# Hybrid decoder step on one core: the local stage, the latent projections and the latent prompt attention as one program, and the order of PE's work within an item of the sample attention

## Chip, cores and metric

One Trainium2 chip (trn2), of which the kernel uses one core. The metric is the device time of one execution in microseconds (us). Engines are named as in the profile: PE (TensorE matmul), PEld (its weight load), DVE (VectorE), ACT (ScalarE), POOL (GpSimd), SP (SyncE, which here issues most transfers).

## The reference

One inference step of one decoder layer. 2048 prompt tokens and 8 samples of 8 new tokens each, with 8192 cached tokens per sample, pass one RMS norm and one input projection. Three kinds of attention follow: **A**, multi-head latent attention (8 heads, latent width 256, shared rotary key of 32); **B**, dilated windows (4 heads of 64, three patterns, 128 keys back each, combined by their softmax sums); **C**, cross attention to 256 memory tokens. The branches are gated, projected and added to the input. The part that the change touches, cut:

```python
q = einsum('bsr,rhd->bshd', rmsnorm(cq, q_a_norm), w_uq)      # 384 -> 8 heads x 96
q_rope = rope(q[..., 64:], pos); ckv = rmsnorm(ckv, kv_a_norm)
o_b = combine_dilations([dilated_prompt(qb, kb, vb, r, w // r) for w, r in ((128, 1), (512, 4), (2048, 16))])
o_c = cross_attend(qc, mk, mv)
# A, prompt: softmax over keys <= own position of (q_lat.ckv + q_rope.krope) * scale, times ckv
# A, sample: the same over 8192 cached tokens (ckv_past, kr_past, by page table) and the 8 new ones
```

## The kernel before

All products are made in 32-bit, and where full precision matters each operand is split into a rounded high part (`_hi`, fp32r) and the difference to it (`_lo`); `mm3` (L97-102) then makes three matmuls: high by high (L100), high by low (L101), low by high (L102).

`program` (L2871-2930) runs stages one behind another. Up to the prompt attention each stage has its own block, and between two blocks all five engines meet at a barrier; the last two stages (sample attention and output projection) share one. `Buffers.release` (L90-94) clears a stage's semaphores and adds a barrier. Within a block each engine has a written order of instructions, and counting semaphores release one engine's work by another's. SP's queue is in order as well: a wait in it holds every later transfer.

**Local stage**, `prompt_windows_and_memory` (L601-977): 64 steps `g` (16 of memory attention, then the patterns d16, d4, d1, 16 each), each on 128 query rows by 4 heads. A loop over `t` runs the parts of a step at fixed distances: `score(t)`, turning of the probabilities `turn(t-2)`, `value(t-3)`, `turn_back(t-4)`. After t = 63 the loop drains for five more turns, with fewer parts in each. SP's loop loads values ahead, and stores results of step t-4 (`store`). `load_ahead` (L703) loads the weights and the first latent chunk of the next stage into `ahead` (class `LatentWeights`, L576), and POOL splits them (`split_ahead`, L762). The last act of SP there is `stored_by(NG)`, a wait for all stores.

**Latent projections**, `prompt_latent_projections` (L1020-1408): four chunks `c` of 512 tokens, and 14 products of 128 x 512 in each: 4 values (`val`), 4 keys (`k_nope`), 6 queries (`Q_ORDER`: four without and two with rotation). Value and key products take six matmuls, query products nine. `acc` has seven banks in turn; ACT and DVE empty them by the table `ON_DVE` (the odd ones of the first eight products and the rotary two, the last in the order, on DVE). A rotary product costs DVE a shuffle, two multiplications and an addition (L1398-1406). SP loads, in this order ahead of chunk 0: the query chunk `load_cq(0)`, eight pieces of the rotary table (2 MB, `rot_loaded`), and then the latent rows of chunk 1. ACT and DVE split the first query chunk at the stage's start, DVE then waits for `rot_loaded` (L1367) ahead of its first eviction. Between products stand `side_step`s for the new sample tokens, which read six small loads. Per chunk SP stores keys, rotary queries (`store_rope`, L1007-1012: four transfers, whose outer dimension is 4 heads) and plain queries (`store_nope`, L1014-1017, one transfer) to memory, where the next stage reads them. Each result buffer is single: it is filled again when its store has landed. In the last chunk SP loads the first unit's keys and queries for the attention (L1145-1150) behind waits for all earlier stores and issues them last; the last stores of plain and rotary queries are left to the next block.

**Prompt attention**, `prompt_latent_attention` (L1411-1863): 32 units, each 256 queries by a pair of heads (8 units to a pair); queries are split by POOL (`split_q`, L1610), from unit 1 on. Unit 0's queries and the keys of the first pair are cast by ACT and subtracted by DVE: queries and key chunk 0 at the stage's start (L1775-1778, L1845-1850), key chunks 1, 2, 3 ahead of the first scores of units 1, 2 and 4 (`CHUNK_BEHIND`, L1548). The list `STEPS` gives one order of score, turn, value and back for all engines. On SP: key chunk 1, queries of unit 2, the last plain-query store, queries of unit 3, key chunk 2, the last rotary store, key chunk 3, and then two units ahead. DVE takes each row's masked scores (L1815), ACT the exponentials (L1755).

**Sample attention**, `sample_attention` (from L1889): 80 items, one after another; 64 of them are past items of 1024 cached tokens. PE's part of an item `n`: `score(n)` (L2133), which for a past item is latent products (L2166, tiles of 128 rows by 64 columns) and then rotary products (L2174, tiles of 64 by 64); `turn_probs(n-1)` (L2178-2186, 64 by 128), which turns the probabilities of the item before; `turn_keys(n+1)` (L2126, 64 by 128); `value(n-1)` (L2209-2225, 128 by 64). Keys are turned and evicted by ACT (L2274) and DVE (L2343), the turned probabilities by ACT (L2280) and DVE (L2374).

```python
2229    for n in range(N):
2230        score(n)
2231        if n:
2232            turn_probs(n - 1)
2233        if n + 1 < N:
2234            turn_keys(n + 1)
2235        if n:
2236            value(n - 1)
```

## Time and profile before

| | |
|---|---|
| median of 3 runs | 1977.24 us (1976.37 to 1979.61) |
| profiled execution | 1976.4 us |
| its span from first to last instruction | 1974.8 us |
| mean granted TensorE clock | 0.985 |
| PE busy | 1890.9 us, 96% |
| DVE, ACT, POOL busy | 53%, 45%, 22% |
| DMA packets | 192238, 270.80 MB, 137 GB/s on the mean |

The page gives busy time as a share of the whole span, and 40 slices of equal length (49 us) with the busy share and the granted clock of each. A view of windows gives the same for any stretch, a view of the timeline gives instructions in order: start, length, engine, line, operation, what it writes and reads, the tile, and in brackets the engine's idle time before it and what released it. `PEq` as a releaser is PE's own sequencer (a barrier or clearing), `SPq` an issue on SP's queue. A time in the text is one from the span's start.

### The profile page before, as it was taken

Reading aid. Unit: us, or ns where it says so; the run is one execution under the profiler, and the core shown is the slowest. Engines: PE = TensorE matmul, PEld = TensorE weight load, DVE = VectorE, ACT = ScalarE, POOL = GpSimd, SP = SyncE. Lnnn points to the kernel's source line nnn. Section 1 sums busy time; section 2 is a strip of 40 time slices with the busy share of each in tenths; the row PEclk is TensorE's granted clock in tenths of the full one; section 3 lists DMA queues with packets and bytes.
Section 4 is the critical chain, followed back from the end, with each engine's and each line's share of the span. In section 5 each row is a group of like instructions: output and inputs, shape, how many; then the busy total and the mean of one; then the engine's idle time right before and its main releaser. Section 6 shows DMA issues by size and latency. Waiting matters only on the chain. (4 is left out here: it accounts for less than half of the span.)

```text
span 1974.8 us, 47163 instructions
## 1 busy us (share of the span) xinstructions
PE 1890.9 (96%) x18076; PEld 1469.0 (74%) x18076; DVE 1047.8 (53%) x3035; ACT 886.8 (45%) x2043; POOL 425.1 (22%) x568
## 2 busy tenths in 40 slices
PE   7999999999989899999999799999999999999998
PEld 6989898766777667776677466666666678888886
DVE  4433434688844477667677455555556753223232
ACT  5222222688822355566556333343434553333332
POOL 0111111355013130134101222222222321211110
PEclk9999999999989899999999799999999999999999
DMA  8534343733465520112001598767784653333331
GB/s 299 155 105 120 100 125 94 216 98 124 141 167 161 162 76 18 46 38 68 26 18 52 169 298 230 222 222 228 241 234 143 207 205 107 102 96 102 119 101 52
DMA packets 192238, 270.80 MB, mean 137 GB/s; under 512 B 37176, under 2 KB 152328, under 8 KB 183128
## 3 DMA queue, kind: packets, MB, share of 16 engines
q1 hardware_dynamic: 172344, 170.27, 30.3%
q0 software_dynamic: 19712, 98.01, 14.4%
q8 instruction: 126, 2.06, 0.4%
q14 instruction: 56, 0.46, 0.1%
HBM read 212.99 MB, written 54.95 MB: 136 GB/s over the span
## 5 line engine op out<-in xcount | busy, mean ns | idle before, releaser
L100 PE MATMUL proj_acc<-proj_w_hi,proj_x_hi 128*128 128x512 f32 (+2 forms) x512 | 183.9, 359 | 10.8 <-DVE proj_x_lo L368 8.2
L101 PE MATMUL proj_acc<-proj_w_lo,proj_x_hi 128*128 128x512 f32 (+2 forms) x512 | 181.8, 355 | 0.0
L102 PE MATMUL proj_acc<-proj_w_hi,proj_x_lo 128*128 128x512 f32 (+2 forms) x512 | 181.8, 355 | 0.0
L1755 ACT ACTIVATE mla_probs<-mla_probs,mla_bias 128x256 f32<-128x256 f32 (+15 forms) x128 | 153.0, 1196 | 11.0 <-DVE mla_bias L1819 7.4
L1815 DVE CUSTOM_DVE_ANT_0 mla_probs<-mla_scores,keep_in_rms 128x512 f32<-128x512 f32 x192 | 124.8, 687 | 59.2 <-PE mla_scores L1673 59.0
L2280 ACT ACTIVATE dec_pT<-dec_outs 128x256 f32<-128x256 f32 x80 | 30.7, 384 | 228.6 <-PE dec_outs L2186 186.1
L2166 PE MATMUL dec_scores<-dec_keysT,sample_q_lat 128*64 128x256 f32 x1024 | 127.0, 388 | 3.3 <-ACT dec_probs L2294 2.2
L2374 DVE COPY dec_pT<-dec_p_turned 128x256 f32<-128x256 f32 x80 | 33.9, 424 | 171.5 <-PE dec_outs L2186 143.6
L100 PEld LDWEIGHTS proj_acc<-proj_w_hi,proj_x_hi 128*128 128x128 f32 x512 | 97.3, 190 | 21.8 <-issue 8.2
L2166 PEld LDWEIGHTS dec_scores<-dec_keysT,sample_q_lat 128*64 128x64 f32 x1024 | 74.4, 139 | 45.1 <-ACT dec_probs L2294 11.6
L2225 PE MATMUL dec_outs<-late_ckv,dec_pT 128*64 128x256 f32 x816 | 101.6, 388 | 5.1 <-DVE dec_pT L2374 4.9
L102 PEld LDWEIGHTS proj_acc<-proj_w_hi,proj_x_lo 128*128 128x128 f32 x512 | 97.2, 190 | 10.7
L101 PEld LDWEIGHTS proj_acc<-proj_w_lo,proj_x_hi 128*128 128x128 f32 x512 | 97.4, 190 | 10.2
L2343 DVE COPY dec_keysT<-dec_turned 128x512 f32<-128x512 f32 (+1 forms) x160 | 96.2, 642 | 10.3 <-PE dec_turned L2126 10.3
L1673 PE MATMUL mla_scores<-mla_k_hi,mla_qn_hi 64*128 64x512 f32 (+3 forms) x320 | 86.6, 455 | 13.5 <-DVE mla_lowest L1815 7.0
L2087 POOL DMA_INDIRECT late_ckv<-in_cache_ckv,sample_rows_of x51 | 48.4, 949 | 236.9 <-PE dec_outs L2225 225.2
L2274 ACT ACTIVATE dec_keysT<-dec_turned 128x512 f32<-128x512 f32 (+1 forms) x160 | 88.9, 557 | 21.9 <-PE dec_turned L2126 19.1
L900 ACT ACTIVATE win_probs<-win_probs,win_rec 128x256 f32<-128x256 f32 (+1 forms) x192 | 86.6, 453 | 21.5 <-DVE win_rec L939 20.9
L269 POOL DMA_DIRECT2D featT<-proj_featT x34 | 26.7, 784 | 309.2 <-DVE proj_featT L429 293.6
L431 DVE COPY proj_featT<-proj_tr 128x512 f32<-128x512 f32 x16 | 11.1, 691 | 151.6 <-PE proj_tr L490 151.6
L1698 PEld LDWEIGHTS mla_turned<-host_ident,mla_probs 64*128 64x128 f32 x2180 | 79.8, 139 | 15.1 <-ACT mla_probs L1755 7.9
L1698 PE MATMUL mla_turned<-host_ident,mla_probs 64*128 64x64 f32 x2180 | 84.1, 224 | 3.9 <-ACT mla_probs L1755 3.9
(466 smaller groups left out, 4933.7 us busy)
## 6 DMA issues: line engine op xcount, KB each, us to landing
win_v_tile<-wv_out SPq DMA_DIRECT2D x75, 128.0 KB
memory_x_raw<-in_xT SPq DMA_DIRECT2D x17, 512.0 KB, 5.1
proj_rows<-in_x SPq DMA_DIRECT2D x17, 512.0 KB, 4.1
featT<-proj_featT POOLq DMA_DIRECT2D x34, 256.0 KB
late_ckv<-in_xT SPq DMA_DIRECT2D x17, 512.0 KB, 6.6
late_ckv<-in_x SPq DMA_DIRECT2D x17, 512.0 KB, 4.3
y_out<-host_buf POOLq DMA_DIRECT2D x16, 512.0 KB, 6.5
dec_k_rows<-in_win_k SPq DMA_DIRECT2D x64, 96.0 KB
```

Of the source, the lines that this page charges most:

```text
L100: pe.matmul(out, lh, rh, start=start, stop=False)
L101: pe.matmul(out, lh, rl, start=False, stop=False)
L102: return pe.matmul(out, ll, rh, start=False, stop=stop)
L900: act.activation(pr, pr, ACT.Exp, bias=low[:, h:h + 1], scale=-1.0, accum_out=total[:, h:h + 1]).then_inc(exp_done, 1)
L1673: mm = pe.matmul(scores[:, at % 3, 0:n], lhs[rows, :], rhs[rows, :], start=a == 0, stop=a == len(parts) - 1)
L1698: mm = pe.transpose(turned[:, r % 2, lane, (kb * 2 * QB + w) * 64:(kb * 2 * QB + w + 1) * 64], probs[rows, u % 2, w, src * P:(src + 1) * P ...
L1755: act.activation(row, row, ACT.Exp, bias=bias[:, at:at + 1], scale=-1.0, accum_out=total[:, at:at + 1]).then_inc(exp_done, 1)
L1815: dve.tensor_tensor_reduce(probs[:, u % 2, w, c * CH:c * CH + wide], scores[:, n % 3, 0:wide], add, -MLA_SCALE, -LOWEST, ALU.add, ALU.min, ...
L2166: pe.matmul(scores[h * Q:(h + 1) * Q, r, 0:HALF * Q], q_lat[:, c, s, :], lanes_of(n, c, r)[:, h * HALF:(h + 1) * HALF, :], start=c == 0, s ...
L2225: mm = pe.matmul(outs[h * Q:(h + 1) * Q, 0:KVL], pT[:, u, j, h * Q:(h + 1) * Q], values[:, h * HALF + j, :], start=j == 0, stop=j == HALF - 1)
L2274: act.activation(lanes_of(n, c, 0), turned_of(n, c, 0), ACT.Copy).then_inc(k_act, 1)
L2343: dve.tensor_copy(lanes_of(n, c, 1), turned_of(n, c, 1)).then_inc(k_dve, 1)
```

## The change

What it does, in the order of the program:

- The three stages become functions that return their per-engine programs, and `program` puts them into one block. No barrier stands between them. `early.release()` goes; POOL clears the early stages' semaphores in the attention, behind unit 12 (`u == NI + 4`). The semaphores of the input projection are cleared (without a barrier) ahead of the block.
- Local stage: SP loads the first query chunk at step 10; POOL casts and subtracts it behind its last staging copy. PE makes the four value products of chunk 0 in the drain, behind `value(61)` to `value(63)` and one turn more, once all scores are masked. SP's wait for the stores goes to where chunk 0's `load_ckv(1)` has been issued.
- Projections: the division of the patterns' shares on DVE (`shares`) goes behind the fourth value product, the wait for the rotary table to the first rotary product. In the last chunk SP issues the first unit's loads ahead of the key store, behind waits for older stores; the third unit's queries behind it; and the last rotary and plain stores in the usual place. ACT casts the first unit's parts ahead of query product 0 (i = 8), DVE subtracts them ahead of product 9; the third key chunk is subtracted behind the last rotation.
- Attention: only key chunk 3 is left in `CHUNK_BEHIND`. SP begins with the queries of unit 3. The order of some buffers in SBUF changes, so that the early casts overwrite nothing in use, and keys are four tiles instead of two.
- Sample attention: for a past item n > 0, `turn_probs(n - 1)` stands between the latent and the rotary products of item n.

The diff, cut to its core ("..." marks what is left out):

```diff
@@ prompt_windows_and_memory: SP @@
+        def wait_stored(sp):
+            stored_by(sp, NG)
...
+                if w == 10:
+                    sp.dma_start(ahead.cq_raw[:], io["featT"].rearrange("(f p) t -> p f t", p=P)[:, FB_CQ:FB_CQ + ahead.QK, 0:ahead.CH]).then_inc(ahead.cq_loaded, 16)
                 if w in (8, 9):
...
-            stored_by(NG)
@@ POOL, behind the loop over the steps @@
+            pool.wait_ge(ahead.cq_loaded, 16)
+            pool.tensor_copy(ahead.cq_hi[:], ahead.cq_raw[:]).then_inc(ahead.cq_high, 1)
+            pool.wait_ge(ahead.cq_high, 1)
+            pool.tensor_tensor(ahead.cq_lo[:], ahead.cq_raw[:], ahead.cq_hi[:].bitcast(F32), ALU.subtract).then_inc(ahead.cq_low, 1)
@@ PE @@
                 if 0 <= t - 3 < NG:
                     value(t - 3)
+                if t == NG:
+                    pe.wait_ge(masked, H_B * NG)
+                if NG <= t < NG + 4:
+                    product(pe, 0, t - NG)
@@ prompt_latent_projections: SP @@
-            load_cq(0)
             for g in range(4):
                 sp.dma_start(cos[32 * g:32 * g + 32, :], io["rotT"][0:32, 0:SEQ]).then_inc(rot_loaded, 16)
...
                 if c == 0:
+                    before.wait_stored(sp)
                     sp.dma_start(cqT[:], feat[:, FB_CQ:FB_CQ + QK, new]).then_inc(new_loaded, 16)
...
-                sp.wait_ge(act_kept, kept_on_act(c, 7))
-                sp.wait_ge(dve_kept, kept_on_dve(c, 7))
                 if c == NCK - 1:
                     sp.wait_ge(ahead.shares_stored, 16)
                     sp.wait_ge(new_valued, DEC_B // 2)
                     sp.wait_ge(k_stored, 16 * c)
-                    sp.wait_ge(qn_stored, 16 * c)
-                    sp.wait_ge(qr_stored, 64 * c)
-                    sp.dma_start(host.k_raw[:, 0:host.CH], io["mla_k"][0:P, 0:host.CH]).then_inc(host.first_loaded, 16)
...
+                    sp.wait_ge(qn_stored, 16)
+                    sp.wait_ge(qr_stored, 64)
+                    first.load(sp)
+                sp.wait_ge(act_kept, kept_on_act(c, 7))
+                sp.wait_ge(dve_kept, kept_on_dve(c, 7))
                 sp.dma_start(io["mla_k"].rearrange("(g p) t -> p g t", p=P)[:, :, cols], k_nope[:]).then_inc(k_stored, 16)
                 if c + 1 < NCK:
                     load_cq(c + 1)
-                if c == NCK - 1:
-                    break
+                else:
+                    sp.wait_ge(qn_stored, 16 * c)
+                    sp.wait_ge(qr_stored, 64 * c)
+                    first.load_third(sp)
                 sp.wait_ge(roped, 2 * c + 2)
-                prompt.store_rope(sp, io, c, qr_stored)
+                prompt.store_rope(sp, io, c, qr_stored if c < NCK - 1 else prompt.qr_last_stored)
                 sp.wait_ge(act_kept, kept_on_act(c, PER - 1))
                 prompt.store_nope(sp, io, c)
@@ PE @@
+                    if c or i >= OUTS_V:
+                        product(pe, c, i)
@@ ACT @@
-            split_cq(0)
...
+                        if c == NCK - 1 and i == OUTS_V + OUTS_K:
+                            first.cast(act)
+                            act.wait_ge(projected, c * PER + i + 1)
@@ DVE @@
-            dve.wait_ge(rot_loaded, 128)
...
+                    if c == NCK - 1 and i == OUTS_V + OUTS_K + 1:
+                        first.split(dve)
                     dve.wait_ge(projected, c * PER + i + 1)
...
                         dve.tensor_copy(val[:, c * 4 + i, :, :].rearrange("p h n -> p (h n)"), src).then_inc(dve_kept, 1)
+                        if c == 0 and i == OUTS_V - 1:
+                            shares()
...
                         if n:
                             dve.wait_ge(roped, n)
+                        else:
+                            dve.wait_ge(rot_loaded, 128)
...
+            first.split_third(dve)
@@ prompt_latent_attention @@
-        CHUNK_BEHIND = {1: 1, 2: 2, 4: 3}
+        LAT_KEYS, LAT_ALL = 3 * 14 + 8, 4 * 14
+        CHUNK_BEHIND = {4: 3}
+
+        def load_first(sp):
+            sp.dma_start(k_raw[:, 0:CH], io["mla_k"][0:P, 0:CH]).then_inc(host.first_loaded, 16)
...
+        def load_third(sp):
+            sp.wait_ge(first_q_ready, 2)
...
+        def cast_first(act):
+            act.wait_ge(host.first_loaded, 48)
+            act.wait_ge(prompt.projected, LAT_KEYS)
+            act.activation(qn_hi[:, 0, :], qn_raw[:, 0, :], ACT.Copy).then_inc(first_q_high, 1)
+            cast_first_k(act, 0)
+            act.activation(qr_hi[:, 0, :], qr_raw[:, 0, :], ACT.Copy).then_inc(first_q_high, 1)
+            cast_first_k(act, 1)
+            cast_first_k(act, 2)
...
-            load_first_k(1)
-            load_q(2)
-            prompt.store_nope(sp, io, SEQ // CH - 1)
             load_q(3)
-            load_first_k(2)
-            prompt.store_rope(sp, io, SEQ // CH - 1, prompt.qr_last_stored)
             sp.wait_ge(masks, 1)
-            load_first_k(3)
+            sp.wait_ge(prompt.k_stored, 16 * SEQ // CH)
+            sp.dma_start(k_raw[:, 3 * CH:], io["mla_k"][0:P, 3 * CH:]).then_inc(first_k_loaded[3], 16)
@@ sample_attention @@
+        def turned_within(n):
+            return n and ITEMS[n][0] == "past"
...
+            if within:
+                turn_probs(n - 1)
             pe.wait_ge(kr_turned, l + 1)
...
             score(n)
-            if n:
+            if n and not turned_within(n):
                 turn_probs(n - 1)
@@ program @@
-            early.release()
+            with nc.Block() as block:
+                @block.sync
+                def _(sp):
+                    windows.sync(sp)
+                    projections.sync(sp, stored, first)
+                    attention.sync(sp)
...
```

## Rows read from the trace of the kernel before

**Rows 1.** The page: busy time of the engines, and PE's granted clock in 40 slices.

```profile
PE 1890.9 (96%) x18076; PEld 1469.0 (74%) x18076; DVE 1047.8 (53%) x3035; ACT 886.8 (45%) x2043; POOL 425.1 (22%) x568
...
PEclk9999999999989899999999799999999999999999
```

**Rows 2.** Windows: length, busy by engine (PE to POOL), granted clock, DMA share, GB/s.

```profile
545.00:550.00 5.00, 3.68 (x52) 2.59 (x48) 2.10 (x5) 0.98 (x2) 0.00 (x0) 1.00 0.16 56
555.00:560.00 5.00, 5.00 (x16) 3.95 (x15) 0.70 (x1) 2.22 (x3) 2.31 (x2) 0.66 1.06 287
565.00:570.00 5.00, 3.02 (x11) 2.15 (x10) 2.26 (x4) 0.60 (x1) 0.00 (x0) 0.86 1.07 281
```

**Rows 3.** Timeline, end of the local stage to chunk 1: start, length, instruction, [idle before, releaser].

```profile
544.71 0.71 PE L849 MATMUL win_turned<-host_ident,win_probs 64*128 64x64 f32 x16 [0.61 <-ACT win_probsT L907]
...
552.73 0.77 PE L100 MATMUL lat_acc<-ahead_wv_hi,ahead_ckv_hi 128*128 128x512 f32 x1 [2.99 <-PEq L646]
...
568.49 0.72 PE L100 MATMUL lat_acc<-lat_cq_hi,ahead_wq_hi 128*128 128x512 f32 x1 [1.98 <-DVE prompt_val L1387]
...
575.69 0.39 PE L100 MATMUL lat_acc<-lat_cq_hi,ahead_wq_hi 128*128 128x512 f32 x1
...
576.37 0.39 PE L100 MATMUL lat_acc<-lat_cq_hi,ahead_wq_hi 128*128 128x512 f32 x1
...
582.49 0.39 PE L100 MATMUL lat_acc<-ahead_wv_hi,ahead_ckv_hi 128*128 128x512 f32 x1
```

**Rows 4.** Timeline, end of the latent projections to unit 3 of the prompt attention.

```profile
677.15 0.42 ACT L1776 ACTIVATE mla_qn_hi<-host_buf 128x256 fp32r<-128x256 f32 x1 [1.76 <-PEq L94]
...
679.58 0.48 PE L1673 MATMUL mla_scores<-mla_k_hi,mla_qn_hi 64*128 64x128 f32 x2 [4.82 <-DVE mla_qr_lo L1850]
...
681.05 0.29 DVE L1815 CUSTOM_DVE_ANT_0 mla_probs<-mla_scores,mla_mask 128x128 f32<-128x128 f32 x1 [1.53 <-PE mla_scores L1673]
...
690.33 0.69 DVE L1803 TENSOR_TENSOR mla_k_lo<-host_buf,mla_k_hi 128x512 fp32r<-128x512 f32 x1 [0.83 <-ACT mla_k_hi L1746]
...
691.69 0.32 PE L1673 MATMUL mla_scores<-mla_k_hi,mla_qn_hi 64*128 64x128 f32 x1 [1.92 <-DVE mla_lowest L1815]
...
696.15 0.47 PE L1673 MATMUL mla_scores<-mla_k_hi,mla_qn_hi 64*128 64x512 f32 x1
```

**Rows 5.** Timeline of issues, releases and rotations around it, with one row of windows.

```profile
650.32 3.65 SPq L1012 DMA_DIRECT2D mla_qr<-prompt_q_rope  x4
...
654.02 1.58 SPq L1017 DMA_DIRECT2D mla_qn<-prompt_q_nope  x1
...
667.51 0.60 ACT L1312 ACTIVATE prompt_q_nope<-lat_acc 128x512 f32<-128x512 f32 x1 [5.71 <-DMA mla_qn<-prompt_q_nope]
...
663.00:665.00 2.00, 2.00 (x10) 1.65 (x10) 0.25 (x1) 0.00 (x0) 0.00 (x0) 1.00 0.26 102
...
666.65 0.73 DVE L1398 STREAM_SHUFFLE lat_swapped<-lat_acc 128x512 f32<-128x512 f32 x1
...
670.73 0.01 DVE L1398 LOAD_MASK_SELECT lat_swapped<-lat_acc  x1 [1.05 <-PE lat_acc L102]
...
672.72 0.69 DVE L1406 TENSOR_TENSOR prompt_q_rope<-lat_turned_cos,lat_turned_sin 128x512 f32<-128x512 f32 x1
...
700.57 0.40 POOL L1618 CAST mla_qn_hi<-host_buf 128x256 fp32r<-128x256 f32 x1 [11.48 <-DMA host_buf<-mla_qr]
```

**Rows 6.** Sample stage: timeline of one item, and PE's waits by releaser (sum, count, longest).

```profile
1250.97 1.16 PE L2126 MATMUL dec_turned<-host_ident,late_ckv 64*128 64x64 f32 x32
...
1252.06 1.95 PE L2225 MATMUL dec_outs<-late_ckv,dec_pT 128*64 128x256 f32 x16
...
1255.66 0.43 PEld L2174 LDWEIGHTS dec_scores<-dec_krT,sample_q_rot 64*64 64x64 f32 x16 [0.38 <-issue]
...
1256.26 0.14 PEld L2186 LDWEIGHTS dec_p_turned<-host_ident,dec_probs 64*128 64x128 f32 x1 [0.17 <-issue]
...
PE dec_outs L2225 <- DVE dec_pT L2374: 7.1, 13, 0.8
```

307 lines of the change are left out of this document (164 added, 143 removed).

## The prediction

> **What bounds the kernel now.** I read the page first: its busy row and its clock row [rows 1]. PE is busy 96% of the span, but the granted clock dips in three places, and a matmul at the low clock counts as busy too. So the question at each place is what PE does there, which busy time alone does not tell. Then I read the windows around the two seams where one block ends and the next begins [rows 2], the timeline of the first seam [rows 3], that of the second [rows 4], the transfers in flight there [rows 5], and last the item of the sample stage [rows 6].
>
> At the first seam PE ends the local stage at 549.74 and starts the latent projections at 552.73: 2.99 us with nothing, and then 1.2 GHz (0.66 of full clock over 555 to 560). A second hole of 1.98 us at 566.5 has another cause: DVE stands before the rotary table's transfer with banks 1 and 3 unread behind it. The clock falls again (0.86, the matmul there 0.72 us long) [rows 2, 3].
>
> At the second seam PE ends at 674.77 and starts scoring at 679.58, 4.82 us later, released by the last of the first unit's splits. PE waits 1.92 us more at 691.69, because the split of the third key chunk stands in ACT's and DVE's queues ahead of the scores [rows 4].
>
> **The change, first seam.** Removed: the barrier; the wait for the table ahead of the first value product's eviction; the load and split of the first query chunk between the stages. Four value products move into the local stage's last steps. Everything PE does from 549.74 to 582.49, where chunk 1 begins, is the 14 products of chunk 0: 8 of six matmuls and 6 of nine, 102 in all. Three matmuls take 0.68 us at full clock (575.69 to 576.37, and ten such steps more make 582.49), so 102 take 23.1 us. They took 32.75. That leaves 9.6 us of holes and slow clock. In the local stage's tail PE also idles 0.61 us at 544.1 and 1.06 us in 545 to 549.74 (5.00 less 3.68 busy less the 0.26 of the hole) [rows 2, 3]; the four products can fill these. Sum: **-11.3 us**, chunk 1 beginning at 571.2. Bounds: if a hole of the size of the second stays with its slow clock (1.98, and some 1.7 for eight matmuls at 0.43 instead of 0.227), -7.6; nothing below -11.3.
>
> What covers it. The first chunk's query cast and difference go to POOL, which has nothing between its last staging copy and the seam; nothing there is late. Its 768 KB load goes on SP's queue in step 10 of the local stage, ahead of step 6's store and of the value loads of later steps. DVE waits on such stores already there; I take 0 and keep +2 as the end. The wait for the masked scores stands on PE at step 64 ahead of the products and of one transposition; it is met 1.5 us before PE comes to it. SP waits for the last local stores only behind chunk 1's load; queued behind that wait are six small loads for the side steps, which need them some 12 us later. Chunk 1's latent load is the next late thing: it now stands behind 2 MB of tables alone, and I expect it at 566 against a need at 571 (third rival).
>
> **Second seam** (times in the frame of before, PE's end at 674.77). Removed: barrier and clearing. Moved: the first unit's loads up, behind chunk 2's stores; the casts to ACT ahead of q product 8's eviction, the differences to DVE ahead of the rotation of product 9. These are two new waits, and what is queued behind them is the rotation, and behind that chunk 3's rotary store, its query store, and the load of unit 3's queries on SP.
> - When do the loads land? Chunk 2's rotary store is issued at 650.32, the query store at 654.02, and the latter lands at 667.51, where ACT's wait ends; in 663 to 665 the queues move 102 GB/s with 0.26 of the engines busy [rows 5]. So a few engines carry the tail, and a load behind it has to wait for them. The three loads' 512 KB have their share on these too: 128 KB at 102 GB/s, 1.3 us. They land at 668.8, not when issued plus 4.
> - From the first cast to the last difference took 2.4 us (677.15 to 679.58), one more difference 0.69 [rows 4]. DVE is free at 671.9. Both rotations cost 5.7 us (666.65 to 673.41, less a wait of 1.05 at 670.73), so they end at 677.6 instead of 673.41 [rows 5].
> - The gain: first masked scores at about 678.7 instead of 681.3, and no wait of 1.92 at 691.69.
> - The loss: the rotary store starts at 677.7, the query store behind it lands 17.2 us later as in chunk 2, at 694.9. Unit 3's queries are loaded behind both, 0.7 us more, and POOL takes 2 us to split them: 697.6. PE starts unit 3 at 696.15 now [rows 4]. In before, a query load behind the last rotary store released POOL only at 700.57, after 11.48 us [rows 5], but there unit 4 was the one that waited, and it was ahead of need. So +1.45. PE idles some 5 us before, so its clock falls again; a hole of 1.98 cost 1.7, part of it hidden since DVE is ahead: +1.0.
>
> Sum: **+2.4 us**. Low bound, if the loads land before 665: the scores follow at once, unit 3's queries are in time: 4.8 us of hole, 1.5 of the 1.92: -6.3. High bound +5: the price of the slow clock twice, and the load as late as 697.
>
> The Trainium skill's page "DMA: Bandwidth & Descriptors", section "Why a DMA increments its semaphore by 16 and not by 1", says that a copy is spread over the largest number of engines up to 16 that divides the outermost dimension of both sides. The rotary store's outer dimension is 4, so by the page it runs on four engines; the share of 0.26 agrees. Were it spread over 16 the low bound would hold.
>
> **Sample stage.** 63 of the 80 items are past items behind another. In each the turn of the previous item's probabilities moves from behind the rotary products to ahead of them. No instruction is added, but the shape of the tiles changes once more: latent, turn, rotary, keys, values instead of latent, rotary, turn and keys (one shape), values. The trace has no 64*128 to 64*64 change. Nearest rows: the weight load waits 0.38 us behind 256-column products, 0.17 us behind 128-column ones (rotary to turn) [rows 6]. Behind 64-column transposes, keys to values take 1.09 us from start to start for 16 pairs at 0.0625: 0.09. The turn is 64 columns wide, so I take 0.10: 63 times, +6.3. Bounds 0 and 0.21 (0.17 and a slower first pair): 0 to +13.2. What it gives: the turned probabilities are ready some 0.5 us earlier (rotary 0.60 less 0.09), and values wait 7.1 us for DVE's copy, in 13 places of up to 0.8 [rows 6]. Nine belong to moved turns; at up to 0.5 each that is -4.0. The maximum on DVE starts no later: it stands behind the same copy now, and that is earlier. Sum **+2.3 us**, range -4 to +9.2.
>
> The page "TensorEngine Tiling (Array Packing)", section "Tiling Modes", in the Trainium skill says that changing the mode drains TensorE, and gives no price. It speaks against this edit, and is the fourth rival.
>
> **Total** -11.3 + 2.4 + 2.3 = -6.6. The profiled execution took 1976.4 us (span 1974.8 and 1.6 around it), so 1969.8; the median of the three runs is 0.8 above, so 1970.6.
>
> **Rivals.**
> 1. The forecast, 1970.6.
> 2. The first unit's loads are not held by the tail of chunk 2's stores. For: they are all 128 partitions wide, and the engines had room. Against: the 17.2 us and the 0.26 share. Seam two gives -6.3: -11.3 - 6.3 + 2.3 = -15.3, 1961.9.
> 3. Chunk 1's latent load is late, PE stands 3.2 us before chunk 1 and runs slow after it (1.7). For: in before a load at this place took some 15 us to land. Against: 1 MB less ahead of it. -1.7, 1975.5.
> 4. Slower: the added change of tiles drains at the dearest row's 0.38, 63 times 23.9, less 4.0: +19.9, with the seams 1988.2. It decides from 0.20 us an item, where the sum is nil. Against: the three widths order the three gaps.
> 5. The joined block does not do away with the first hole: PE still stands about 3.0 us for the engines to come together, then 2.7 slow. -0.9, 1976.3.
>
> **Numbers.** 0.58, 0.22, 0.10, 0.04, 0.06. Range: from 1.9 under rival 2 to just over rival 5, 1960 to 1977, leaving out rival 4 and the edges. About 0.2% (4.0 us, 1973.3) is what a measurement of this kernel can tell from no change. Faster: 0.85 of the forecast (0.49), rival 2, a quarter of rival 3: 0.74. Slower: rival 4 and edges, 0.06. Same 0.20.
>
> **What would show it.** Right: no PE hole over 1 us between the last local transposition and chunk 1, clock 1.0 throughout; ACT's first unit cast 1 to 2 us after the query store of chunk 2 lands; POOL waiting for unit 3's queries with PE waiting for POOL; a weight-load gap near 0.07 us ahead of the rotary products, and few waits of values for the copy. Wrong: the first cast well ahead of that landing (rival 2); a wait of PE on the latent difference (rival 3); a rotary gap of 0.2 or more (rival 4).

## The result: 1959.84 us, 0.8% faster, and more of it from the sample stage than forecast

| | before | changed |
|---|---|---|
| median on the same chip | 1978.18 us | 1959.84 us (lowest 1958.84) |
| ratio, 95% interval | | 0.9918, 0.9895 to 0.9941 |
| profiled execution | 1976.4 us, span 1974.8 | 1959.79 us, span 1958.1 |
| mean granted clock | 0.985 | 0.990 |

One of the changed kernel's four executions took 3651 us and is left out of the ratio; the other three lie within 1.1 us, and no trace shows what made that one slow. The forecast was 6.6 us less than before; it is 18.3 by the two medians, or 16.2 by the ratio. Sign right, size off by a factor of about 2.5. The ratio times the earlier median, 1977.24, gives 1961.0, just inside the range.

**First seam.** The page of the changed kernel (busy row, clock row) and then its windows over the seam: length, busy by engine from PE to POOL, granted clock, DMA share, GB/s.

```profile
PE 1887.9 (96%) x18076; PEld 1466.6 (75%) x18076; DVE 1055.5 (54%) x3034; ACT 887.8 (45%) x2042; POOL 431.5 (22%) x569
...
PEclk9999999999999899999999899999999999999999
```

```profile
545.00:550.00 5.00, 5.00 (x46) 3.88 (x47) 1.87 (x4) 0.98 (x2) 0.00 (x0) 1.00 0.15 52
...
555.00:560.00 5.00, 5.00 (x24) 4.14 (x23) 1.66 (x3) 0.69 (x2) 0.00 (x0) 1.00 1.02 216
...
565.00:570.00 5.00, 5.00 (x24) 4.14 (x23) 1.99 (x4) 2.03 (x3) 0.00 (x0) 1.00 1.05 293
```

They answer to [rows 1, 2]: PE is busy through all three windows, at full clock, where it had 3.68, 5.00 at 0.66, and 3.02. PE's busy time hardly changed (1890.9 to 1887.9); what went is idle time and matmuls at half clock. In the timeline, against [rows 3], the products stand among the local stage's last steps, and chunk 1 begins at 569.91:

```profile
537.13 1.14 PE L846 MATMUL win_scores<-win_kT,win_qT 64*128 64x256 f32 x8
...
550.40 0.39 PE L104 MATMUL lat_acc<-ahead_wv_hi,ahead_ckv_lo 128*128 128x512 f32 x1
...
550.64 0.38 PE L883 MATMUL win_back<-host_ident,win_outT 128*128 128x128 f32 x2
...
569.91 0.39 PE L102 MATMUL lat_acc<-ahead_wv_hi,ahead_ckv_hi 128*128 128x512 f32 x1
```

The last local scores stood at 538.46 in the kernel before, so from there to chunk 1 it is 32.78 us instead of 44.03 (582.49): 11.25 less, the forecast's 11.3.

**Second seam.** The timeline of all engines, in the order of time:

```profile
655.87 0.42 ACT L1601 ACTIVATE mla_q_parts<-host_buf 128x256 fp32r<-128x256 f32 x1 [6.92 <-DMA host_buf<-mla_qr]
...
661.84 0.33 PE L1731 MATMUL mla_scores<-mla_even_k_hi,mla_q_parts 64*128 64x128 f32 x2
...
664.34 1.04 DVE L1423 TENSOR_TENSOR prompt_q_rope<-lat_turned_cos,lat_turned_sin 128x512 f32<-128x512 f32 x1
665.30 0.68 DVE L1596 TENSOR_TENSOR mla_even_k_lo<-host_buf,mla_even_k_hi 128x512 fp32r<-128x512 f32 x1
665.41 3.65 SPq L1024 DMA_DIRECT2D mla_qr<-prompt_q_rope  x4
665.91 0.28 DVE L1857 CUSTOM_DVE_ANT_0 mla_probs<-mla_scores,mla_mask 128x128 f32<-128x128 f32 x1
...
666.25 0.58 PE L1731 MATMUL mla_scores<-mla_even_k_hi,mla_q_parts 64*128 64x256 f32 x1 [3.46 <-DVE mla_bias L1857]
...
682.52 0.69 DVE L1873 COPY prompt_q_nope<-mla_turned 128x512 f32<-128x512 f32 x1 [1.01 <-DMA mla_qn<-prompt_q_nope]
683.18 0.40 POOL L1674 CAST mla_q_parts<-host_buf 128x256 fp32r<-128x256 f32 x1 [18.34 <-DMA host_buf<-mla_qr]
...
685.35 0.80 PE L1731 MATMUL mla_scores<-mla_even_k_hi,mla_q_parts 64*128 64x512 f32 x2 [4.46 <-POOL mla_q_parts L1679]
```

The reader is to see a chain, each link in a bracket: the first casts wait for the loads (655.87), the rotation ends late (665.38), the rotary store goes out at 665.41, the plain store behind it lands at 682.5, POOL gets unit 3's queries at 683.18, and PE, 4.46 us idle, starts unit 3 at 685.35. The windows around the two holes have the clock:

```profile
665.00:670.00 5.00, 3.54 (x20) 2.60 (x20) 2.49 (x11) 1.97 (x8) 0.00 (x0) 0.50 0.17 35
670.00:675.00 5.00, 4.76 (x35) 4.22 (x36) 2.70 (x9) 1.29 (x4) 0.00 (x0) 0.53 0.68 194
...
680.00:685.00 5.00, 0.89 (x28) 0.75 (x24) 2.17 (x7) 3.83 (x8) 1.82 (x4) 0.99 0.28 95
685.00:690.00 5.00, 4.65 (x22) 3.01 (x24) 1.31 (x4) 0.38 (x1) 3.97 (x9) 0.50 0.17 54
```

1.2 GHz (0.50) is granted for two stretches here, each behind a hole; the kernel before had one at this seam (0.50 over 680 to 685, 0.69 over 685 to 690).

**Sample stage.** PE's waits from 1125 to 1560 and one row of the weight loads' (PEld); sum, count, longest. The kernel before:

```profile
PE dec_outs L2225 <- DVE dec_pT L2374: 6.0, 11, 0.8
PE dec_scores L2148 <- ACT dec_keysT L2274: 3.4, 8, 0.7
...
PE dec_scores L2166 <- ACT dec_probs L2294: 1.5, 8, 0.3
...
PEld dec_scores L2166 <- ACT dec_probs L2294: 10.5, 26, 0.7
```

and the changed one:

```profile
PE dec_scores L2195 <- ACT dec_probs L2338: 2.6, 7, 0.4
...
PE dec_outs L2269 <- DVE dec_pT L2418: 0.6, 1, 0.6
PE dec_scores L2208 <- ACT dec_probs L2338: 0.5, 1, 0.5
PE dec_scores L2189 <- ACT dec_keysT L2318: 0.3, 1, 0.3
...
PEld dec_scores L2208 <- ACT dec_probs L2338: 3.8, 9, 0.9
```

In PE's own rows, waits for DVE's copy of the turned probabilities, for ACT's key casts and for ACT's exponentials were 10.9 us and are 4.0. Why the second row is nearly gone is seen where a window item follows a past one. Before, with the past item's rotary products at 1187.67:

```profile
1189.23 0.42 DVE L2374 COPY dec_pT<-dec_p_turned 128x256 f32<-128x256 f32 x1 [2.56 <-PE dec_outs L2186]
...
1189.57 0.68 DVE L2367 TENSOR_REDUCE dec_gmax<-dec_scores 128x1 f32<-128x512 f32 x1
...
1190.74 0.67 ACT L2294 ACTIVATE dec_probs<-dec_scores,sample_nb 128x512 f32<-128x512 f32 x1
...
1191.40 0.58 ACT L2274 ACTIVATE dec_keysT<-dec_turned 128x512 f32<-128x512 f32 x1
...
1192.08 1.94 PE L2148 MATMUL dec_scores<-dec_keysT,dec_q_win 128*64 128x512 f32 x8 [0.38 <-ACT dec_keysT L2274]
```

and changed, with the rotary products at 1176.29:

```profile
1177.49 0.69 DVE L2411 TENSOR_REDUCE dec_gmax<-dec_scores 128x1 f32<-128x512 f32 x1 [0.46 <-PE dec_scores L2218]
...
1178.66 0.67 ACT L2338 ACTIVATE dec_probs<-dec_scores,sample_nb 128x512 f32<-128x512 f32 x1
...
1179.33 0.58 ACT L2318 ACTIVATE dec_keysT<-dec_turned 128x512 f32<-128x512 f32 x1
...
1180.01 1.94 PE L2189 MATMUL dec_scores<-dec_keysT,dec_q_win 128*64 128x512 f32 x8
```

DVE copies the turned probabilities first and then takes the maximum. Before, the maximum began 1.90 us behind the rotary products' start, held by the copy; now 1.20, held by the products themselves. ACT's exponentials follow the maximum, and ACT's last key cast follows them, so the window item's scores, which need these keys, start 3.72 us behind the rotary products instead of 4.41.

The weight loads' row looks larger, 10.5 us against 3.8, but a wait there costs only what it delays of the matmuls behind it. Between two past items, before and changed:

```profile
1353.25 1.95 PE L2225 MATMUL dec_outs<-late_ckv,dec_pT 128*64 128x256 f32 x16
1355.03 1.49 PEld L2166 LDWEIGHTS dec_scores<-dec_keysT,sample_q_lat 128*64 128x64 f32 x16 [0.29 <-ACT dec_probs L2294]
1355.03 1.95 PE L2166 MATMUL dec_scores<-dec_keysT,sample_q_lat 128*64 128x256 f32 x16
```

```profile
1339.07 1.95 PE L2269 MATMUL dec_outs<-late_ckv,dec_pT 128*64 128x256 f32 x16
1340.63 1.66 PEld L2208 LDWEIGHTS dec_scores<-dec_keysT,sample_q_lat 128*64 128x64 f32 x16
1340.84 1.90 PE L2208 MATMUL dec_scores<-dec_keysT,sample_q_lat 128*64 128x256 f32 x16
```

The wait of 0.29 us is gone, and the latent products start 1.77 us behind the values instead of 1.78.

### The profile page after: what moved, and what is told of

The parts are those of the page before. It is cut to its first block and busy times, and to the rows that moved or that the text cites. A ratio compares the mean times of both kernels' runs of the same rounds, so it can differ in the third digit from the quotient of the medians.

```text
span 1958.1 us, 47133 instructions
## 1 busy us (share of the span) xinstructions
PE 1887.9 (96%) x18076; PEld 1466.6 (75%) x18076; DVE 1055.5 (54%) x3034; ACT 887.8 (45%) x2042; POOL 431.5 (22%) x569
## 3 DMA queue, kind: packets, MB, share of 16 engines
q8 instruction: 126, 2.06, 0.4%
## 5 line engine op out<-in xcount | busy, mean ns | idle before, releaser
L1857 DVE CUSTOM_DVE_ANT_0 mla_probs<-mla_scores,keep_in_rms 128x512 f32<-128x512 f32 x192 | 124.8, 688 | 64.6 <-PE mla_scores L1731 64.2
L1731 PE MATMUL mla_scores<-prompt_kr_parts,mla_q_parts 64*128 64x512 f32 (+3 forms) x640 | 136.7, 373 | 0.0
L2208 PE MATMUL dec_scores<-dec_keysT,sample_q_lat 128*64 128x256 f32 x1024 | 124.0, 382 | 3.0 <-DVE dec_keysT L2387 1.8
L104 PEld LDWEIGHTS proj_acc<-proj_w_hi,proj_x_lo 128*128 128x128 f32 x512 | 97.3, 190 | 10.7
L2387 DVE COPY dec_keysT<-dec_turned 128x512 f32<-128x512 f32 (+1 forms) x160 | 96.3, 642 | 8.7 <-PE dec_turned L2164 8.6
L1731 PE MATMUL mla_scores<-mla_even_k_hi,mla_q_parts 64*128 64x512 f32 (+3 forms) x320 | 81.8, 420 | 14.9 <-DVE mla_lowest L1857 5.8
```

The source lines that it names most:

```text
L104: return pe.matmul(out, ll, rh, start=False, stop=stop)
L1731: mm = pe.matmul(scores[:, at % 3, 0:n], lhs[rows, :], rhs[rows, :], start=a == 0, stop=a == len(parts) - 1)
L1857: dve.tensor_tensor_reduce(probs[:, u % 2, w, c * CH:c * CH + wide], scores[:, n % 3, 0:wide], add, -MLA_SCALE, -LOWEST, ALU.add, ALU.min, ...
L2208: pe.matmul(scores[h * Q:(h + 1) * Q, r, 0:HALF * Q], q_lat[:, c, s, :], lanes_of(n, c, r)[:, h * HALF:(h + 1) * HALF, :], start=c == 0, s ...
L2387: dve.tensor_copy(lanes_of(n, c, 1), turned_of(n, c, 1)).then_inc(k_dve, 1)
```

## The experiments

Twelve kernels ran, each against the kernel before on the same chip. Single executions scatter by several us, most of it in the local stage, which no experiment's edit touches; the change itself puts one 768 KB load into it. So each trace is also read by stretches of PE's timeline: **A** from the last local scores to the last latent product, **B** from there to the first matmul of the sample stage, **C** from that to the last output product. "Local" is first to last local scores. All times are from start to start.

| kernel | local | A | B | C | median, us | ratio, 95% interval |
|---|---|---|---|---|---|---|
| before | 175.2 | 135.9 | 432.1 | 860.3 | | |
| changed | 174.2 | 124.4 | 435.4 | 853.3 | 1959.84 | 0.9918 [0.9895, 0.9941] |
| e1 turn undone | 178.4 | 124.8 | 433.1 | 860.7 | 1966.08 | 0.9949 [0.9931, 0.9967] |
| e2 turn alone | 177.7 | 136.6 | 433.4 | 853.5 | 1971.75 | 0.9980 [0.9964, 0.9996] |
| e3 turn where short | 172.7 | 124.6 | 434.3 | 851.7 | 1957.79 | 0.9916 [0.9896, 0.9937] |
| e4 fourth and plain first | 173.9 | 123.5 | 426.2 | 853.9 | 1952.99 | 0.9893 [0.9873, 0.9914] |
| e5 changed again | 175.8 | 124.0 | 434.4 | 855.2 | 1960.82 | 0.9913 [0.9892, 0.9934] |
| e6 no fill | 171.6 | 126.4 | 433.5 | 854.3 | 1964.07 | 0.9934 [0.9913, 0.9956] |
| e7 table wait ahead | 180.0 | 134.7 | 432.7 | 856.0 | 1972.81 | 0.9969 [0.9956, 0.9983] |
| e8 both | 177.2 | 123.4 | 427.9 | 852.2 | 1953.51 | 0.9870 [0.9846, 0.9893] |
| e9 fourth early only | 177.0 | 124.7 | 427.4 | 851.8 | 1954.80 | 0.9894 [0.9873, 0.9914] |
| e10 rotary store spread | 177.2 | 124.8 | 424.6 | 853.8 | 1952.17 | 0.9882 [0.9860, 0.9903] |
| e11 POOL takes keys | 173.2 | 123.9 | 424.9 | 851.3 | 1948.25 | 0.9861 [0.9838, 0.9884] |
| e12 all | 177.2 | 123.4 | 422.5 | 854.5 | 1947.88 | 0.9847 [0.9829, 0.9865] |

Over the traces that share a stage as it was or as it is: A is 136.3 (two) and 124.1 (ten), 12.2 less. B is 432.7 (two) and 433.9 (six), 1.2 more. C is 860.5 (before and e1) and 854.0 (eight), 6.5 less. Sum -17.5; the two ratios of the changed kernel, 0.9918 and 0.9913, say -16.2 and -17.2. The load in the local stage, which the forecast took at 0 with +2 kept as the end, shows nothing: 176.4 us on the mean of the two traces without it, 175.7 of the twelve with it.

### e1, e2: is it the turn?

```diff
         def turned_within(n):
-            return n and ITEMS[n][0] == "past"
+            return False
```

> The changed kernel with the turn of the probabilities back behind the rotary products; all else as changed. Theory A (the sample stage's edit pays): from the first sample matmul to the last the changed kernel runs in 5.3 us less than the one before (1106.42 to 1562.72 against 1096.92 to 1547.91). If the moved turn is the cause, the stage goes back to 456 us here, the 13 waits for the copy of the turned probabilities (7.1 us) return, and the time is 4 to 6 us above the changed kernel, about 1965. Rival B (the forecast's own term): the edit costs 2 us, the gain comes from the earlier gathers at the stage's start; then this kernel is 2 us faster than the changed one, about 1958, with the stage's first gather waits (3.3 us in all) as in the changed kernel. Between them: only run to run scatter, within 1 us of 1959.8.

For e2 the kernel before took `if turned_within(n): turn_probs(n - 1)` between its latent and rotary products, and nothing else.

> The kernel before with nothing changed but the place of the turn in past items. Theory A: some 5 us faster than before, ratio 0.9975, about 1973, and the wait of values for the copy falls from 7.1 us to under 1. Rival B: 2 us slower, 1979. In both a past item's own steps get longer by 0.16 us, since the trace of the changed kernel has 0.40 us from the turn to the rotary products and 1.15 from keys to values where before had 1.09, and the gap between latent products and whatever follows stays 0.38.

Undone, C is 860.7, that of before, and the 7.1 us of waits for the copy are back. Alone, C is 853.5, that of the changed kernel, and the ratio says 3.9 us faster (0.8 to 7.1). Theory A stands: stretch C follows the place of the turn, put in alone and taken out alone. Rival B, the earlier gathers at the stage's start, can have a share of 1 us or so (the table under e3). The ratio of e1 is 0.0031 above the changed kernel's, 6 us.

### e3: only where the next item is short

```diff
-            return n and ITEMS[n][0] == "past"
+            return 0 < n < N - 1 and ITEMS[n][0] == "past" and ITEMS[n + 1][0] != "past"
```

> The changed kernel with the turn moved only in past items whose next item is a window or rest item (16 items at most), since those are where values waited 0.7 us for the copy, or the next item's scores 0.4 us for the keys. If the cost is 0.16 us for each moved turn and the gain sits at those places, this saves 47 times 0.16, 7.5 us, less the small waits between past items (0.18 and 0.34 at the weight load) that come back: 3 to 7 us faster than the changed kernel, 1953 to 1957. Rival: the waits between past items are worth as much as the change of tiles, and the time is within 1 us of 1959.8.

The time decides nothing (0.9916 against 0.9918 and 0.9913), and the expected 3 to 7 us did not come. C is 852.4 on the mean of the four kernels with this edit (e3, e8, e11, e12), 1.6 less than with all turns moved. The fourteen traces tell where the moved turn pays. This is PE's time from an item's first scores to the next item's, items 4 to 77 (counted from 0, as `n` in the kernel), in us, as a sum over the items of a kind, with mean and range by the place of the turn:

| items | unmoved: before, e1 | all 63 moved: eight | 16 moved: four |
|---|---|---|---|
| 16 past, next is window or rest | 96.3, 96.3 | 91.2 (90.7 to 92.1) | 91.6 (91.3 to 92.0) |
| 29 past, between past items | 170.4, 172.2 | 173.6 (172.4 to 174.5) | 170.2 (169.9 to 170.5) |
| 13 past, behind window or rest, next is past | 75.1, 75.3 | 73.7 (73.1 to 74.6) | 74.9 (74.1 to 75.8) |
| 16 window and rest | 75.7, 75.5 | 76.0 (75.7 to 76.6) | 76.1 (75.7 to 76.6) |
| stretch C ahead of item 4 | 35.0, 33.7 | 33.0 (32.5 to 33.9) | 32.8 (32.6 to 33.0) |
| stretch C behind item 77 | 407.8, 407.6 | 406.5 (406.1 to 407.0) | 406.9 (406.4 to 407.4) |

The gain is in the 16 items that e3 keeps moved, 5 us. Where an item stands between past items the moved turn costs 2.3 us in 29, 0.08 each, and e3 has that back. It has it back although the weight loads' waits for the exponentials are all there again:

```profile
PEld dec_scores L2208 <- ACT dec_probs L2338: 10.4, 26, 0.7
```

So that row, the largest of the dependency waits in the weight loads' table, is worth at most the 1.2 us that separate the last two columns in the third row. Ahead of item 4 no turn is moved in the four kernels of the last column either, and they are as fast there as the eight: the 1.4 us there is not the turn's, and e1's 33.7 lies within the range of the eight.

### e4, e9: which half of the order on SP

```diff
@@ load_third
+            sp.wait_ge(q_ready, 2)
+            sp.dma_start(qn_raw[:, 1, :], io["mla_qn"][0:P, 3 * CW:4 * CW]).then_inc(q_loaded[1], 16)
+            sp.dma_start(qr_raw[:, 1, :], io["mla_qr"][0:P, 3 * CW:4 * CW]).then_inc(q_loaded[1], 16)
@@ prompt_latent_attention, sync
-            load_q(3)
             sp.wait_ge(masks, 1)
@@ projections, last chunk (e4 only): the plain store ahead of the rotary one
+                if c == NCK - 1:
+                    sp.wait_ge(act_kept, kept_on_act(c, PER - 1))
+                    prompt.store_nope(sp, io, c)
                 sp.wait_ge(roped, 2 * c + 2)
...
```

> The changed kernel with the queries of unit 3 loaded behind those of unit 2, ahead of chunk 3's stores, and the plain-query store ahead of the rotary one in the last chunk. Theory: PE's wait of 4.46 us for POOL at 685.35 is owed to that load standing behind the rotary and plain stores; here POOL splits unit 3's queries by 668, the wait is gone, and with it part of the slow clock (0.75 and 0.91 in the windows 680 to 700): 5 to 7 us faster than the changed kernel, about 1954. Rival: the turned probabilities need the plain-query buffer, whose store then lands as late as before (682.5) or DVE stays the bound there; then PE waits for the turned probabilities instead and the gain is under 2 us.

> The fourth experiment's first half alone: unit 3's queries loaded ahead of chunk 3's stores, the stores in the changed kernel's order (rotary, then plain). Theory: the lateness has two heads. The queries are then ready by 670, but ACT and DVE reuse the plain-query buffer for turned probabilities and wait for its store, which stays behind the rotary store and lands at 682.5 (the changed kernel's DVE waits there, 1.01 us, with no cost yet). PE is held by that instead: of the 7 us that both halves gave in the attention (426.2 and 427.9 against 433 to 435) this half gives 1 to 3. Rival: the load alone was the matter, and the stretch from the last latent product to the first sample matmul is 427 as with both.

B falls from 433.9 to 426.2 with both and to 427.4 with the load alone. So the load's place in SP's queue was nearly all of it, and my theory for e9, that the plain buffer would hold PE next, fell. Of e4's timeline:

```profile
666.66 0.58 PE L1737 MATMUL mla_scores<-mla_even_k_hi,mla_q_parts 64*128 64x256 f32 x1 [3.83 <-DVE mla_bias L1863]
...
668.24 0.40 POOL L1680 CAST mla_q_parts<-host_buf 128x256 fp32r<-128x256 f32 x1 [3.77 <-PE mla_scores L1737]
```

POOL no longer waits for a transfer but for PE to free a buffer, 15 us earlier; the first hole, 3.83 us, is about as it was. The wait of 4.46 us is gone, and the gain of 6 to 8 us is larger than it; the second stretch at 1.2 GHz went too (the granted clock is 1.00 from 675 to 700, where the changed kernel has 0.50 over 685 to 690 and 0.82 over 690 to 695).

### e5: the changed kernel again

> The changed kernel itself, on the chip of the next three, as their reference: 16 to 18 us faster than the kernel before, ratio 0.992. By stages I expect the numbers of its first trace within 1 us: last local scores to last latent product 124.4 us, from there to the first sample matmul 435, from that to the last output matmul 853.

Ratio 0.9913, A and B within about 1 us, C 1.9 above the first trace, outside of what was expected: C of one kernel scatters by some 2 us from trace to trace, so one trace does not resolve 1.

### e6, e7: the parts of the first seam

```diff
@@ e6: local stage, PE
-                if NG <= t < NG + 4:
-                    product(pe, 0, t - NG)
@@ e7: projections, DVE
+            dve.wait_ge(rot_loaded, 128)
             for c in range(NCK):
...
-                        else:
-                            dve.wait_ge(rot_loaded, 128)
```

In e6 the four products are made at the head of the projections.

> The changed kernel with the four value products of chunk 0 behind the local stage's last step, as before, still in one block. The forecast put the idle time that they fill at 1.67 us (0.61 and 1.06); so the stretch from the last local scores to the last latent product goes from 124.4 to 126.1 us. Rival: the changed kernel's tail lasts 13.9 us with 5.4 us of products in it, where it lasted 11.3 without, so they hide 2.8 of themselves there; then it is 127.2. A second rival, the barrier's 2.99 us comes back in another form: 129 or more.

> The changed kernel with DVE's wait for the rotary table ahead of its first eviction, as before, while products and all else stay as changed. The forecast priced that wait at 1.98 us and 1.7 of slow clock: 3.7 slower than the changed kernel, stretch 128.1. Rival: the table's transfers are issued at 552 to 555 in both kernels, and land at about 565, but the products are 10 us earlier, so PE comes to bank 1 at 557.5 and stands some 8 us, plus slow clock: stretch 133 to 135, time 8 to 10 us above.

e6: A is 126.4, 2.3 above the mean of 124.1, between the 1.67 of the forecast and the rival's 2.8; A of the ten kernels scatters from 123.4 to 124.8, so it does not decide between them. The second rival, 129 or more, fell. So the joined block and the moved wait give 9.9 of the 12.2 us without the filled tail. e7: A is 134.7, 10.6 above, and the ratio 0.0056 above e5's, 11 us; the rival holds. The wait kept its place in time while everything in front of it moved up:

```profile
570.88 1.29 DVE L1401 COPY prompt_val<-lat_acc 128x512 f32<-128x512 f32 x2 [12.58 <-DMA lat_sin<-in_rotT]
571.62 0.29 PEld L102 LDWEIGHTS lat_acc<-ahead_cq_hi,ahead_wq_hi 128*128 128x128 f32 x1 [8.22 <-DVE prompt_val L1401]
571.62 0.80 PE L102 MATMUL lat_acc<-ahead_cq_hi,ahead_wq_hi 128*128 128x512 f32 x1 [7.79 <-DVE prompt_val L1401]
```

The table landed 27.8 us behind the last local scores here (543.09 to 570.88), and 29.3 in the kernel before (538.46 to 567.74). What the moved wait is worth depends on what else is done: 3.7 us by the forecast's reading of the trace of before, 10.6 once the barrier is gone. Without the moved wait, all else gives only 1.6 of the 12.2 us. The wait moved with the barrier kept was not run.

### e8: e3 and e4 together

> The edits of the third and fourth experiments together: unit 3's queries and plain queries first, and the turn moved only in the 16 past items whose next is no past item. They lie in different stages, so their gains add: 8 us in the prompt attention and 1.5 to 3 in the sample stage, 10 us below the changed kernel, ratio to before 0.987. Rival: the gathers at the sample stage's start are tied to the attention's end, and part of it is lost in a longer wait for the first pages: under 8.

Ratio 0.9870 against 0.9913 on the same chip, 8.5 us, where 10 were expected. B is 427.9, C 852.2. PE waited 4.5 us for its first pages here and 3.3 in the changed kernel's trace, but this wait runs from 2.2 to 5.2 us over the fourteen traces, so the rival is neither shown nor ruled out.

### e10: is the rotary store on few engines?

```diff
-                sp.dma_start(io["mla_qr"]...[g, d][:, :, cols], self.q_rope[:, g, :]).then_inc(done, 16)
+                for h in range(4):
+                    sp.dma_start(io["mla_qr"]...[g, d, h][:, cols], self.q_rope[32 * h:32 * h + 32, g, :]).then_inc(done, 16)
```

(the counts waited for are four times as high)

> The changed kernel with each of the four transfers of a rotary store cut into four, of 32 rows each, so that the outer dimension of a transfer is 32 and not 4: 16 transfers for each chunk. Theory: 1 MB went out over few engines (102 GB/s at 0.26 busy), so what stands behind it landed 17.1 us after the store's issue (665.4 to 682.5). Spread out, the plain store behind lands 10 to 12 us after, of which 7 are SP's sixteen issues; POOL gets unit 3's queries about 5 us earlier, PE's wait of 4.46 us is gone and the attention is 430 us instead of 434, and ahead of it ACT's first cast comes 2 to 4 us earlier. Rival: the few engines are not the cause, the landing is as late or later for the longer issue, attention 434 to 437.

The same three microseconds, 668 to 671, behind the start of the rotary store, in the changed kernel and then in e10:

```profile
668.00:671.00 3.00, 2.76 (x14) 2.05 (x16) 1.34 (x6) 1.08 (x4) 0.00 (x0) 0.50 0.23 82
```

```profile
668.00:671.00 3.00, 2.41 (x18) 1.54 (x14) 1.54 (x7) 1.35 (x6) 0.41 (x1) 0.63 0.53 137
...
677.00:680.00 3.00, 2.42 (x44) 1.91 (x41) 1.91 (x7) 0.93 (x2) 0.31 (x1) 1.00 0.97 311
```

Bytes and order are the same, but the share goes from 0.23 (3.7 of the sixteen engines) to 0.53. SP's sixteen issues take 7.37 us now and probably set the pace; once they are out, the queues move 311 GB/s. POOL has unit 3's queries 13.3 us after the store's first issue (666.35 to 679.69) instead of 17.8 (665.41 to 683.18). B is 424.6, better than the expected 430. PE still waits 1.51 us for POOL, and nobody waits for the plain store, so the trace does not say when it landed. The spread helps ahead of the seam too: ACT's first cast comes 8.1 us before the last latent product starts (656.74 to 664.86), 5.7 in the changed kernel (655.87 to 661.52), since chunk 2's stores are out of its way sooner. The casts come earlier by that, and the first hole is 1.27 us instead of 3.46. That is a part of the gain on which the expectation had put no number. The Trainium skill's rule of the page "DMA: Bandwidth & Descriptors" (section "Why a DMA increments its semaphore by 16 and not by 1"), four engines for an outer dimension of 4 and sixteen for 32, agrees with these runs: 3.7 engines' worth of work with 4, and 0.53 and then 0.97 of the sixteen with 32.

### e11, e12: the hole that was left

```diff
@@ DVE, split_first and split_third: chunks 1 and 2 left out
-            split_first_k(dve, 1)
-            split_first_k(dve, 2)
@@ POOL, behind split_q(2)
+                    for c in (1, 2):
+                        pool.wait_ge(first_k_high, c + 1)
+                        pool.tensor_tensor(even_k_lo[:, cols], k_raw[:, cols], even_k_hi[:, cols].bitcast(F32), ALU.subtract).then_inc(pool_k_ready, 1)
```

(e11 is e8 with this; PE and SP wait for POOL's semaphore in place of DVE's where chunks 1 and 2 are needed)

> The eighth experiment's kernel with the differences of key chunks 1 and 2 on POOL, behind its split of unit 2, instead of on DVE around the last rotations. Theory: the last hole at this seam (3.2 to 3.8 us at 666) is DVE's chain of differences (2.6), two rotations (6.2) and one more difference ahead of the first masked scores; taking 1.4 us out of it makes the hole 1.4 us shorter: attention 1.4 to 2.5 us less than 427.9, ratio to before 0.986. Rival: rotations wait for their products anyway (0.44 us idle between them), or POOL hands over the third chunk late and the wait turns up at unit 2: within 0.5 us of the eighth.

e12 is e11 with the stores of e10.

> The eleventh experiment's kernel with the rotary stores cut into sixteen transfers as in the tenth. Theory of one shared wait: both edits bring unit 3's queries in time, and that can be gained once; what is left of the spread store is the earlier landing of unit 4's queries and a lighter tail, so attention is 423 to 425 (424.9 and 424.6 alone) and the ratio to before 0.985 to 0.986. Rival: they act on different waits and add up, attention 421 or less, ratio under 0.984. A second rival, SP's sixteen issues now stand ahead of other loads that were in time: 426 or more.

The hole at the second seam in e11 and in e12:

```profile
663.63 0.39 PE L1745 MATMUL mla_scores<-mla_even_k_hi,mla_q_parts 64*128 64x256 f32 x1 [2.06 <-DVE mla_bias L1871]
```

```profile
665.69 0.38 PE L1746 MATMUL mla_scores<-mla_even_k_hi,mla_q_parts 64*128 64x256 f32 x1 [0.36 <-DVE mla_bias L1872]
```

e11: 2.06 us, 1.1 to 1.8 less than in e8 and e4, and B 3.0 less than e8's: slightly over the expected 1.4 to 2.5. The clock still falls there, to 0.50 over 665 to 670; in e12 it stays at 1.00. e12: B is 422.5, 2 us below each alone: between "one shared wait" (423 to 425) and "they add up" (421), and that is not settled. Both run faster than the kernel before and the changed one: e12 has 0.9847 (0.9829 to 0.9865), e11 0.9861, where the changed kernel has 0.9918 and 0.9913; the medians are 1947.88 and 1948.25. e11 and e12 can't be told apart by time.

## Why the prediction was right in its seams and wrong in its size

**First seam, right.** Forecast -11.3, with chunk 1 as its mark: -11.25 in the trace, and -12.2 for the whole stretch A over ten traces. The 102 matmuls went through at full speed without a hole; the latent load of chunk 1 was in time (rival 3 fell: DVE's difference for chunk 1 is at 568.01, need 569.91), and so did rival 5. Two terms inside were not what they seemed: the tail's 1.67 us is 2.3 by e6 (a difference within the scatter of A), and the table's wait, 3.7 in the kernel before, is worth 10.6 in the new surroundings (e7). The sum was safe since it was made as "everything, less the work that stays", not as a sum of waits.

**Second seam, the chain right, the price near.** In the frame of before the forecast had (all less 12.6, the shift at chunk 1): loads landed 668.8, so 656.2; measured 655.87. Rotations end 677.6, so 665.0; 665.38. First masked scores 678.7, so 666.1; 665.91. Plain store landed 694.9, so 682.3; 682.5. Unit 3's queries ready 697.6, so 685.0; 685.35. Every link is within 0.4 us. Unit 3's start lost 1.8 us (696.15 less 12.6 makes 683.55), forecast 1.45. The net term was +2.4; B is 1.2 higher over six traces and 3.3 in the one shown, so its size is not known better than that. e4 shows that the loss was avoidable: the load one place further up in SP's queue is worth 6 to 8 us.

**Sample stage, wrong: +2.3 forecast, -6.5 measured.** This is the step that failed, and it failed in its gain. The cost, "63 times 0.10, +6.3", held. By the medians over past items, rotary products start 0.39 us behind the turn's start, where keys started 0.30 behind it, and values start 1.14 behind the keys instead of 1.12: 0.11 an item, and the table under e3 has 0.08.

The gain, "nine belong to moved turns; at up to 0.5 each that is -4.0", was too small in two ways. First, the copy. In seven of the eight past items ahead of a rest item the values waited 0.66 to 0.82 us for it, more than the cap of 0.5. On the mean of the six of them that also follow a past item (traces of before and changed) values now start 0.68 us sooner behind the keys, and the rest item's scores start 0.25 later behind the values, held by the exponentials: over eight items -5.4 and +2.0. Second, the earlier maximum. The forecast had it, "the maximum on DVE ... stands behind the same copy now, and that is earlier", but used it only to exclude a loss, and put the gain at nothing. The exponentials are 0.70 us earlier with it, and so are ACT's key casts behind them. PE's own table had 3.4 us of scores waiting for these casts ahead of window items; there, on the mean of seven, scores start 1.93 us behind the values instead of 2.32, over eight items -3.1. Behind a rest item, whose value products are short, the next latent products start 1.58 us behind them instead of 1.84, over eight items -2.1. Together these are -8.6, where the forecast had -4.0; less a cost of 5 to 7, some -2 to -4, and the table under e3 has -3.8 for items 4 to 77. The rest of stretch C's 6.5, 1.4 us ahead of item 4 and 1.3 behind item 77, has no cause shown.

Rival 4 asked the right question: the tiles' change does cost, but 0.08 to 0.11 an item is well under the 0.20 that it set as its turning point, and near the forecast's 0.10. The rule of the Trainium skill (page "TensorEngine Tiling (Array Packing)", section "Tiling Modes"), that a change of mode drains TensorE, fits the 0.09 us by which the products behind the turn start later; that it is a drain no trace here shows by itself. With the gain of 8.6 the edit pays up to 8.6 / 63 = 0.14 an item.

**Ranges and rivals.** Rival 2, loads not held by the stores, came nearest in time (1961.9) and did not happen: the first cast stood behind chunk 2's stores as forecast. That the time still fell just inside the range, whose low end was set from rival 2, is luck; it came there by the sample stage, a path that no rival had.

## What to carry to other kernels

- Where an engine has a queue of its own for a part of its work, as weight loads have, a long wait there need not cost anything: compare the starts of the matmuls behind it with and without it. Here a row of 10.5 us was worth little, and rows of 6.0 and 3.4 us in the matmuls' own table were the gain.
- When items are of several kinds, price an edit by kind. One mean over 63 items hid that 16 gain 5 us and 29 lose 2.
- When a step is moved, follow what is freed on each engine behind it until it releases the engine that sets the pace. "No later" is half an answer; ask how much earlier.
- A wait is worth what stands before it at the time. Taking a barrier out moves all that is ahead of the next wait up to it, and a transfer's issue has to move with its need. In SP's queue a load that is due soon goes ahead of a store that nobody is waiting for.

## What the runs showed of the hardware

- A store of 1 MB whose transfers have an outer dimension of 4 holds what stands behind it for some 17 us, with 0.23 of the DMA engines busy (82 GB/s); the same bytes with outer dimension 32 let it pass in 13, of which 7.4 were issues (e10 against the changed kernel).
- One more change of tile shape in an item, from turns (64 by 128) to rotary products (64 by 64), started these 0.09 us later. Weight loads lose 0.39 us behind the latent products, 256 columns wide, whether rotary products follow (before) or the turn (changed).
- The granted clock fell to 0.50 (1.2 GHz) behind holes of 3.46 and 4.46 us, behind one of 7.79 in e7 and one of 2.06 in e11; in e10, with a hole of 1.27, it was 0.63 over 668 to 671; in e12, whose hole is 0.36, it stayed at 1.00 from 660 to 685.
- The local stage lasted from 171.6 to 180.0 us in fourteen traces, whatever the kernel. DVE waits there for stores of its own results (8.7 us in the trace of before, 10.7 in the longest, e7), but what makes the rest vary was not looked into. It is more than most edits here are worth, and the reason to compare stretches and not single times.
